# Seven block products in place of eight in both up projections, with GpSimd making the low parts of the weight blocks and their sums

## The chip, the cores and the metric

One core of one Trainium2 chip runs the whole program. The metric is the device time of one execution in microseconds: 2602.4 us before the change (median of 3 runs, 2601.3 to 2602.51).

## The reference, cut to what matters

The program computes two transformer-like blocks, one behind the other, on 1024 tokens of width 1024. The change touches the two feed-forward parts, the first of the first block and the second of the second:

```python
def _conv_ffn(h, w_up, conv_w, conv_b, w_down):      # h: 1024 x 1024, w_up: 1024 x 5632
    up = h @ w_up
    up = causal_depthwise_conv_width_3(up, conv_w) + conv_b
    val, gate = jnp.split(up, 2, axis=-1)
    return (jax.nn.silu(gate) * val) @ w_down

def conv_ffn(h, w_up, conv_w, conv_b, w_down, grid_rows):
    a, g = jnp.split(h @ w_up, 2, axis=-1)           # 2816 columns each
    a = dwconv3x3(a as 16 rows of 64 tokens, conv_w) + conv_b
    return (jax.nn.gelu(a, approximate=False) * g) @ w_down
```

## The kernel before, in words

Activations lie transposed, 128 features on the partitions and tokens along the free axis. A large product is made from bf16 parts: each fp32 matrix is split into a high part (rounded to bf16) and a low part (the rest), and `PASSES` multiplies high by high, high by low and low by high (line 189), three matmuls of 128 x 128 weights by 512 tokens for each 128 rows of the inner dimension. The moving parts of the normed input lie in `hT`.

**The up projection** (`Ffn`, line 1978) runs 22 units. Unit j makes 128 features of the first half of the columns (s = 0) and 128 of the second (s = 1), for 1024 tokens in two halves: four PSUM banks of a unit, two units in turn. A unit is 4 x 8 x 3 = 96 matmuls. Its weights (1 MB, two DMAs issued by SyncE, SP) come into one raw buffer; ScalarE (ACT) makes the high parts (L2051), VectorE (DVE) the low parts (L2084), into one of two buffers, and only then is the raw buffer loaded again. GpSimd (POOL) does nothing in it.

Behind the matmuls of a unit ACT writes the centre tap with bias out of PSUM (L2127, L2156), DVE adds the other taps one after another (`conv_causal`, L2137, four of them; `conv_grid`, L2170, eight), ACT applies Silu or Gelu (L2147, L2179), DVE multiplies (L2149, L2181), ACT writes the high part of the gated product (L2063) and DVE the low part (L2097). Each engine runs its list in order; `act_unit` and `dve_unit` (L2053, L2086) write the order out, and loops (`Fori`) run over pairs of units. PE starts the first halves of units 0 and 1 while the norm of the second token half is still being made (`pe_first_half`), and then their second halves (`pe_rest`). The norm (`Norm`, L512) scales on DVE (L693), shifts and rounds on ACT (L643), and subtracts on DVE (L705); the scaled values of the second feed-forward live in four small rotating buffers.

**The down projection** (`DownByHalves`, L1821) follows: 16 units of 22 x 3 = 66 matmuls. Unit 0's raw weights are loaded while the up projection ends (`load_first`), unit 1's and all later ones' into the region of `hT` when the up projection has read it. One raw buffer again: SP issues unit u's load when unit u-1's low part is made (L1872), ACT and DVE split it (L1893, L1899). Units 0 and 1 run their first 21 of 22 row blocks, then wait for the last unit of the up projection. `update` adds the product to the residual `xT`, which stays in place all the time.

Of the kernel before, what the change touches and what calls it, by code (L numbers as in the profile page):

```python
# [111 lines left out]
ARENA = 31488  # L112


class Kernel:


    def __init__(self, nc, ins, out, ctx):
# [393 lines left out]
class Norm:  # L512
# [85 lines left out]
    def act_square(self, act, i, a, b, t):  # L598
# [4 lines left out]
        if self.dst is None and self.split is not None and i == self.tiles:  # L603
            act.wait_ge(self.ready, self.tiles)
# [82 lines left out]
    def dve_scale(self, dve, i, n, a, b, t):  # L687
# [3 lines left out]
        if self.dst is None and t >= 4:  # L691
            dve.wait_ge(self.ready, i - 3)
# [1127 lines left out]

class DownByHalves:  # L1821
# [6 lines left out]
    def __init__(self, k, w_name, gate, second_banks=4):  # L1828
# [19 lines left out]
    def first_splits(self):  # L1848

        n = FT - 1 - self.FIRST  # L1850
        return [(self.raw_first[0], self.w_even[0]), (self.raw_first[1][:, 0:n, :], self.w_even[1][:, :, 0:n, :]),
                (self.raw_first[1][:, n:, :], self.last_row)]

    def first_hi(self, act, f):

        act.wait_ge(self.first_loaded, 32)
        act.wait_ge(f.made[0], FT // 2 + 1)
        for i, (raw, parts) in enumerate(self.first_splits()):
            if i == 1:
                act.wait_ge(f.done[0], FT // 2 + 1)  # L1860
# [1951 lines left out]
```

## Time and profile before

| what | before |
|---|---|
| median of 3 runs | 2602.4 us |
| span of the profiled execution, first to last instruction | 2597.6 us |
| what lies around the span, taken against the median | 4.8 us |
| PE busy | 2484.4 us (96%) |
| DVE, ACT, POOL busy | 1622.0, 886.6, 26.8 us |
| up projection 1, units 2 to 21 | 541 to 955.1 us |
| up projection 2, units 2 to 21 | 1928.1 to 2342.8 us |

The profile gives no time of the profiled execution but its span; the 4.8 us around it are the difference from the median. PE is TensorE's matmul queue; L200 is the matmul line of the helper `split_matmuls`, L1917 that of the down projection.

### The profile page before, as it was taken

What the parts mean: (1) busy time and instruction counts of PE and PEld (TensorE: products, weight loads), DVE (VectorE), ACT (ScalarE), POOL (GpSimd) and SP (SyncE); (2) the same over time, 40 slices, a digit from 0 to 9 for tenths busy, and PEclk for the clock granted to TensorE, in tenths of its full rate; (3) what the DMA queues carried; (4) which work ended last, traced back from release to release, by engine and by line L of the source; (5) the groups of instructions that cost most, each with busy time, mean ns of one, the idle gap of its engine ahead of it and who ended that gap; (6) DMA issues with size and microseconds to landing.
All of it is one profiled execution on the core that took longest, in us unless ns stands there. A gap on an engine that the chain in (4) does not pass through costs nothing. (4 is left out here: it accounts for less than half of the span.)

```text
span 2597.6 us, 39539 instructions
## 1 busy us (share of the span) xinstructions
PE 2484.4 (96%) x16809; PEld 1336.3 (51%) x16809; DVE 1622.0 (62%) x2112; ACT 886.6 (34%) x1061; POOL 26.8 (1%) x60
## 2 busy tenths in 40 slices
PE   7999889999999999999999999979989999999997
PEld 4457664444444444444767776764434444444443
DVE  6688747544444443645477878786766777774243
ACT  5118316332233232323354544452332222222121
POOL 0010000010000000000000000000000000000000
PEclk9999999999999999999999999999999999999999
DMA  9127563111111124343210000021101211113442
GB/s 328 31 73 235 192 212 131 33 49 49 48 48 48 48 77 111 106 120 130 56 31 18 25 26 25 18 97 50 33 17 52 61 49 48 48 55 106 112 112 87
DMA packets 302918, 207.37 MB, mean 80 GB/s; under 512 B 11296, under 2 KB 298174, under 8 KB 302143
## 3 DMA queue, kind: packets, MB, share of 16 engines
q1 hardware_dynamic: 301910, 205.08, 26.3%
q8 instruction: 105, 1.72, 0.3%
q10 hardware_dynamic: 873, 0.32, 0.1%
q14 instruction: 30, 0.25, 0.0%
HBM read 191.22 MB, written 13.64 MB: 79 GB/s over the span
## 5 line engine op out<-in xcount | busy, mean ns | idle before, releaser
L200 PE MATMUL ps<-hT,arena 128*128 128x512 bf16 (+1 forms) x6240 | 1337.3, 376 | 13.3 <-DVE hT L705 4.9
L200 PEld LDWEIGHTS ps<-hT,arena 128*128 128x128 bf16 x6240 | 609.1, 98 | 739.0 <-issue 17.1
L1917 PE MATMUL ps<-arena 128*128 128x512 bf16 x2112 | 458.7, 379 | 3.0 <-DVE arena L1899 3.0
L1917 PEld LDWEIGHTS ps<-arena 128*128 128x128 bf16 x2112 | 206.3, 98 | 252.2 <-DVE arena L1899 5.3
L2170 DVE SCALAR_TENSOR_TENSOR arena<-ps,vec,arena 128x945 f32<-128x945 f32 (+2 forms) x176 | 215.1, 1222 | 70.1 <-ACT arena L2156 50.7
L2137 DVE SCALAR_TENSOR_TENSOR arena<-ps,vec,arena 128x1023 f32<-128x1023 f32 (+1 forms) x88 | 106.8, 1276 | 177.8 <-ACT arena L2127 177.8
L1899 DVE TENSOR_TENSOR arena<-hT,arena 128x2816 bf16<-128x2816 f32 (+2 forms) x44 | 93.7, 2157 | 164.8 <-ACT arena L1893 164.6
L1893 ACT ACTIVATE arena<-hT 128x2816 bf16<-128x2816 f32 (+2 forms) x44 | 77.8, 1798 | 240.1 <-DMA hT<-w_down_dram 112.6
L2988 PE MATMUL ps<-arena 128*128 128x128 f32 (+1 forms) x896 | 103.2, 272 | 21.6 <-DVE arena L3309 21.6
L2084 DVE TENSOR_TENSOR arena<-hT,arena 128x2048 bf16<-128x2048 f32 x44 | 100.9, 2292 | 28.1 <-ACT arena L2051 27.8
L2988 PEld LDWEIGHTS ps<-arena 128*128 128x128 f32 (+1 forms) x896 | 98.5, 187 | 25.6 <-DVE arena L3309 24.0
L2127 ACT ACTIVATE arena<-ps,vec 128x1024 f32<-128x1024 f32 x44 | 50.6, 1200 | 173.5 <-PE ps L200 173.5
L2179 ACT ACTIVATE arena<-arena 128x1024 f32<-128x1024 f32 x22 | 23.2, 1056 | 227.5 <-DVEq L2174 227.5
L2097 DVE TENSOR_TENSOR arena<-arena 128x1024 f32 (+1 forms) x44 | 53.9, 1225 | 59.9 <-ACT arena L2063 59.9
L2051 ACT ACTIVATE arena<-hT 128x2048 bf16<-128x2048 f32 x44 | 83.3, 1894 | 8.1 <-DMA hT<-w_up_dram 8.1
L3326 DVE COPY_PREDICATED arena<-masks,ps 128x512 f32<-128x512 uint32 x56 | 49.9, 890 | 56.1 <-PE ps L2988 55.4
L3128 ACT ACTIVATE arena<-arena 128x1024 f32<-128x1024 f32 x56 | 58.4, 1053 | 73.7 <-DVE arena L3300 53.0
L3073 ACT ACTIVATE arena<-ps 128x1024 f32<-128x1024 f32 (+1 forms) x48 | 36.2, 755 | 123.9 <-PE ps L200 112.2
L605 ACT ACTIVATE arena<-xT 128x512 f32<-128x512 f32 x64 | 39.8, 630 | 110.9 <-DVE xT L568 54.0
L200 PE MATMUL ps<-arena,hT 128*128 128x128 bf16 (+1 forms) x1152 | 76.0, 228 | 0.9 <-PEq L160 0.9
L200 PEld LDWEIGHTS ps<-arena,hT 128*128 128x128 bf16 x1152 | 72.9, 98 | 3.7 <-issue 1.2
L1068 PE MATMUL ps<-arena 128*128 128x512 f32 x160 | 71.6, 599 | 1.7 <-ACT arena L645 1.1
(421 smaller groups left out, 2468.9 us busy)
## 6 DMA issues: line engine op xcount, KB each, us to landing
xT<-ada_w_dram SPq DMA_DIRECT2D x24, 1024.0 KB, 5.9
hT<-w_up_dram SPq DMA_DIRECT2D x44, 512.0 KB, 5.0
hT<-ffn_up_dram SPq DMA_DIRECT2D x44, 512.0 KB, 5.0
hT<-w_down_dram SPq DMA_DIRECT2D x30, 704.0 KB, 7.1
hT<-ffn_down_dram SPq DMA_DIRECT2D x30, 704.0 KB, 6.9
arena<-w_in_dram SPq DMA_DIRECT2D x33, 512.0 KB, 3.9
xT<-w_mod_dram SPq DMA_DIRECT2D x16, 1024.0 KB, 6.1
arena<-w_mod_dram SPq DMA_DIRECT2D x8, 1024.0 KB, 19.2
```

The source lines that it names most:

```text
L200: last = pe.matmul(out, lhs(a, kt), rhs(b, kt, i), start=start and kt == 0 and (a, b) == (0, 0), stop=stop and kt == n_k - 1 and (a, b) == ...
L1068: last = pe.matmul(k.ps[:, 2 * p + half, :], exact[n][:, kt, :], h[:, kt, half * HALF:(half + 1) * HALF], start=kt == 0, stop=kt == KD - 1)
L1893: last = act.activation(parts[0], raw, ACT.Copy)
L1899: last = dve.tensor_tensor(parts[1], raw, parts[0], ALU.subtract)
L1917: last = pe.matmul(self.bank(u), self.part(u, a, kt), self.g[:, b, kt, cols], start=kt == 0 and (a, b) == (0, 0), stop=kt == FT - 1 and (a ...
L2051: act.activation(self.w[:, b, :, 0], self.raw, ACT.Copy).then_inc(self.hi[b], 1)
L2084: dve.tensor_tensor(self.w[:, b, :, 1], self.raw, self.w[:, b, :, 0], ALU.subtract).then_inc(self.lo[b], 1)
L2097: dve.tensor_tensor(self.g[:, 1, 2 * i + b, :], c[0], self.g[:, 0, 2 * i + b, :], ALU.subtract).then_inc(self.done[b], 1)
L2137: last = eng.scalar_tensor_tensor(c[s][:, lag:T], p[s][:, 0:T - lag], w[:, tap, s, bass.ds(j, 1)], c[s][:, lag:T], ALU.mult, ALU.add)
L2170: eng.scalar_tensor_tensor(to, src[:, r0 + di:r1 + di, c0 + dj:c1 + dj], w[:, 3 * (di + 1) + dj + 1, bass.ds(j, 1)], to, ALU.mult, ALU.add ...
L2988: return pe.matmul(out[rows, columns], chunk[:, rows], chunk[:, columns], start=True, stop=True)
L3128: act.activation(v, v, ACT.Exp).then_inc(exp_done, 1)
```

## The change

Both up projections become classes of their own, `CausalFfn` and `GridFfn`, on a common `Ffn`, with every loop written out. Units 0, 1 and 2 stay plain (96 matmuls). From unit 3 on (`PLAIN = 3`, 19 units) the 256 x 1024 weights and the 1024 x 1024 input are taken as 2 x 2 blocks, and the four output banks are made by seven block products of 4 x 3 matmuls each, 84 in all, by Winograd's form: three sums of weight blocks (S1, S2, S4), one difference in place of a block (S3), and four combinations of input blocks (T1 to T4), made once. Partial results are passed on inside PSUM: ACT copies the bank of product 1 over the next bank (`seed_12`), copies that one on after product 6 (`seed_21`), keeps product 5 in SBUF, and DVE adds it twice (`finish_22`, `finish_12`). TensorE makes product 4 of unit u behind product 1 of unit u+1. GpSimd makes T1 to T4 of both norms from the normed values, which now stay whole in SBUF (`place`), and for each of the 19 units the four sums of weight blocks and both low parts. `xT` is stored to HBM before the up projection, its place holds the convolution's buffers and T1 and T2, and it is loaded back when the up projection ends.

```diff
+    def load(self, sp, u):                     # one raw buffer
+        if u >= 1:
+            sp.wait_ge(self.a_lo, u)
+        for s in range(2):
+            sp.dma_start(self.raw[...], self.src[u, s]).then_inc(self.loaded, 16)
+    def sync(self, sp, down):
+        for u in range(2, FT):
+            self.load(sp, u)
+        sp.wait_ge(self.a_lo, FT)
+        sp.wait_ge(self.s_lo, FT - self.PLAIN)
+        down.load_first(sp)
+        sp.wait_ge(self.made, FT)
+        down.load(sp, 1)
+        sp.dma_start(self.k.xT[:, 0:4, :], self.x_mid[:, 0:4, :]).then_inc(down.x_home, 16)
+        sp.wait_ge(self.done, FT)
+        sp.dma_start(self.k.xT[:, 4:KD, :], self.x_mid[:, 4:KD, :]).then_inc(down.x_home, 16)
...
+        for u in range(self.PLAIN, FT):        # PE; product: 12 matmuls
+            pe.wait_ge(self.a_lo, u + 1)
+            pe.wait_ge(self.free0, u - 1)
+            self.product(pe, c11, u, self.A11, ...).then_inc(self.multiplied_out, 1)
+            if u > self.PLAIN:
+                fourth_product(u - 1)          # waits for added (22) of u-1
+            pe.wait_ge(self.s_lo, n)
+            pe.wait_ge(self.free1, u - 1)
+            self.product(pe, c22, u, self.S1, ..., True, range(0, 2))
+            pe.wait_ge(self.copied, self.copy_count(u, "1 to 12"))
+            self.product(pe, c12, u, self.S2, ...).then_inc(self.multiplied_out, 1)
+            self.product(pe, c11, u, self.A12, ..., False)
+            self.product(pe, c22, u, self.S1, ..., False, range(2, 4)).then_inc(self.multiplied_out, 1)
+            pe.wait_ge(self.copied, self.copy_count(u, "12 to 21"))
+            self.product(pe, c21, u, self.S3, ..., False).then_inc(self.multiplied_out, 1)
+            self.product(pe, c12, u, self.S4, ..., False).then_inc(self.multiplied_out, 1)
...
+    def pool(self, pool, norm):
+        pool.wait_ge(norm.normed, 2 * KD)
+        pool.tensor_tensor(self.t1, v12, v11, ALU.subtract).then_inc(self.combined, 1)
+        pool.tensor_tensor(self.t2, v22, self.t1, ALU.subtract).then_inc(self.combined, 1)
+        pool.tensor_tensor(v11, self.t2, v11, ALU.subtract).then_inc(self.combined, 1)
+        pool.tensor_tensor(v21, v21, self.t2, ALU.subtract).then_inc(self.combined, 1)
+        for u in range(self.PLAIN, FT):
+            pool.wait_ge(self.loaded, 32 * (u + 1))
+            pool.tensor_tensor(sums[:, 0], raw[:, self.A21], raw[:, self.A22], ALU.add).then_inc(self.summed, 1)
+            pool.tensor_tensor(raw[:, self.S3], raw[:, self.A11], raw[:, self.A21], ALU.subtract).then_inc(self.summed, 1)
+            pool.tensor_tensor(sums[:, 1], sums[:, 0], raw[:, self.A11], ALU.subtract).then_inc(self.summed, 1)
+            pool.tensor_tensor(sums[:, 2], raw[:, self.A12], sums[:, 1], ALU.subtract).then_inc(self.summed, 1)
+            self.lo_a(pool, u)                 # 128x2048, behind ACT's hi_a
+            self.lo_s(pool, u)                 # 128x1536, behind ACT's hi_s
...
+    def act(self, act, down):
+        self.hi_t(act, 1)                      # T1's high part; waits for both spills
+        self.hi_t(act, 2)
+        for u in range(FT):
+            if self.strassen(u):
+                act.wait_ge(self.added, self.added_count(u, 12))
+            else:
+                act.wait_ge(self.made, u + 1)
+            self.first_centre(act, u)
+            if self.strassen(u + 1):
+                self.seed_12(act, u + 1)
+            act.wait_ge(self.made, u + 1)
+            self.second_centre(act, u)
+            if u + 2 < FT:
+                self.hi_a(act, u + 2)          # waits for made(u) and for the sum S3 of u+2
+            if self.strassen(u + 2):
+                self.hi_s(act, u + 2)
...
+            if self.strassen(u + 1):
+                self.seed_21(act, u + 1)
+            self.activate(act, u)
+            if self.strassen(u + 1):
+                self.keep_p5(act, u + 1)
+            act.wait_ge(self.multiplied, u + 1)
+            act.activation(self.g[:, 0, u, :], self.conv_of(u, 0), ACT.Copy).then_inc(self.g_hi, 1)
+    def dve(self, dve, down):
+        self.lo_t(dve, 1)
+        for u in range(FT):
+            if self.strassen(u):
+                self.finish_12(dve, u)
+            self.taps(dve, u)
+            if 2 <= u + 2 < self.PLAIN:
+                self.lo_a(dve, u + 2)
+            if u == FT - 2:
+                down.first_lo(dve)
+            if u == FT - 1:
+                down.split_lo(dve, 1)
+            dve.wait_ge(self.acted, u + 1)
+            self.multiply(dve, u)
+            if u == 0:
+                self.lo_t(dve, 2)
+            if self.strassen(u + 1):
+                self.finish_22(dve, u + 1)
+            dve.wait_ge(self.g_hi, u + 1)
+            dve.tensor_tensor(self.g[:, 1, u, :], ...).then_inc(self.done, 1)
+            if u == 0:
+                self.lo_t(dve, 3)
+            if u == self.PLAIN - 1:
+                self.lo_t(dve, 4)
```

In the stages, `f.load` and `f.spill` (2 MB of `xT` to `x_mid` for each token half) stand in SP's list behind the mixer's weights, and `down.update` waits for `x_home`. GpSimd's building of the masks of a later stage moves behind the first down unit.

## Rows read from the trace of the kernel before

**Rows 1.** The page: busy time of each engine, share of the span, instructions.

```profile
PE 2484.4 (96%) x16809; PEld 1336.3 (51%) x16809; DVE 1622.0 (62%) x2112; ACT 886.6 (34%) x1061; POOL 26.8 (1%) x60
```

**Rows 2.** The page: the chain that ended last, shares of the span by line.

```profile
PE ps L200 19%; PE ps L1917 7%; DVE arena L2170 1%; DMA hT<-ffn_down_dram 1%; PE ps L589 1%; PE ps L3530 1%; DVE arena L1899 0%; ACT arena L1893 0%; PE ps L3572 0%; DVE arena L693 0%; DVE hT L3702 0%; DVE arena L2084 0%; DVE hT L705 0%; ACT
```

**Rows 3.** The chain of waits in order of time: start us, us, what.

```profile
1949.10 393.87 PE ps L200 x1824
```

**Rows 4.** Two stretches: length, busy us (times) by engine, granted clock, DMA share, GB/s.

```profile
541.00:955.11 414.11, 414.11 (x1920) 187.72 (x1919) 194.41 (x144) 126.03 (x103) 0.00 (x0) 1.00 0.19 52
...
1900.00:1907.00 7.00, 6.12 (x16) 1.45 (x17) 7.00 (x12) 3.96 (x6) 0.00 (x0) 0.59 0.01 2
```

**Rows 5.** GpSimd's groups by shape: busy us, mean ns of one, idle before.

```profile
L2617 POOL TENSOR_SCALAR_AFFINE_SELECT masks<-masks 128x64 f32<-128x64 f32 x28 | 9.9, 352 | 1.9
...
L1056 POOL MEMSET arena<- 128x7168 f32 x1 | 6.1, 6076 | 89.3 <-PE ps L1083 89.3
...
L1040 POOL MEMSET arena<- 64x1 f32 x1 | 0.1, 92 | 0.1
```

**Rows 6.** VectorE's groups by shape.

```profile
L2170 DVE SCALAR_TENSOR_TENSOR arena<-ps,vec,arena 128x945 f32<-128x945 f32 x88 | 105.7, 1202 | 59.0 <-ACT arena L2156 50.7 <-DVE arena L2170 1.4
...
L2084 DVE TENSOR_TENSOR arena<-hT,arena 128x2048 bf16<-128x2048 f32 x44 | 100.9, 2292 | 28.1 <-ACT arena L2051 27.8
...
L2097 DVE TENSOR_TENSOR arena<-arena 128x1024 f32 x36 | 44.1, 1225 | 50.9 <-ACT arena L2063 50.9
...
L705 DVE SCALAR_TENSOR_TENSOR hT<-arena,mod,hT 128x512 bf16<-128x512 f32 x48 | 34.7, 747 | 0.0
...
L1717 DVE TENSOR_TENSOR arena<-ps,arena 128x512 f32<-128x512 f32 x4 | 2.8, 688 | 4.5 <-PE ps L1572 4.5
```

**Rows 7.** ScalarE's groups by shape.

```profile
L2051 ACT ACTIVATE arena<-hT 128x2048 bf16<-128x2048 f32 x44 | 83.3, 1894 | 8.1 <-DMA hT<-w_up_dram 8.1
...
L2156 ACT ACTIVATE arena<-ps,vec 128x1024 f32<-128x1024 f32 x22 | 26.5, 1204 | 70.4 <-PE ps L200 70.4
...
L2179 ACT ACTIVATE arena<-arena 128x1024 f32<-128x1024 f32 x22 | 23.2, 1056 | 227.5 <-DVEq L2174 227.5
...
L643 ACT ACTIVATE hT<-arena,mod 128x512 bf16<-128x512 f32 x64 | 45.2, 719 | 36.5 <-DVE arena L693 36.5
...
L1379 ACT ACTIVATE arena<-ps 128x512 f32<-128x512 f32 x28 | 15.2, 594 | 10.4 <-PE ps L1329 10.4
```

**Rows 8.** The page: DMA issues, times, KB each, median us from issue to landing.

```profile
hT<-ffn_up_dram SPq DMA_DIRECT2D x44, 512.0 KB, 5.0
...
hT<-w_down_dram SPq DMA_DIRECT2D x30, 704.0 KB, 7.1
...
xT<-x_kept SPq DMA_DIRECT2D x2, 4096.0 KB, 13.0
```

**Rows 9.** Timeline, start of up projection 2: start us, us, engine, line [idle before].

```profile
1906.13 2.07 DVE L705 SCALAR_TENSOR_TENSOR hT<-arena,mod,hT 128x512 bf16<-128x512 f32 x3
...
1914.30 1.21 ACT L2156 ACTIVATE arena<-ps,vec 128x1024 f32<-128x1024 f32 x1 [7.33 <-PE ps L200]
...
1915.54 10.03 DVE L2170 SCALAR_TENSOR_TENSOR arena<-ps,vec,arena 128x945 f32<-128x945 f32 x8 [7.33 <-ACT arena L2156]
...
1928.06 57.25 PE L200 MATMUL ps<-hT,arena 128*128 128x512 bf16 x263 [3.44 <-DVE arena L2084]
```

**Rows 10.** Timeline, start of down projection 1.

```profile
955.11 57.14 PE L1917 MATMUL ps<-arena 128*128 128x512 bf16 x264
...
962.89 2.55 ACT L1893 ACTIVATE arena<-hT 128x2816 bf16<-128x2816 f32 x1 [5.28 <-DMA hT<-w_down_dram]
...
965.48 3.09 DVE L1899 TENSOR_TENSOR arena<-hT,arena 128x2816 bf16<-128x2816 f32 x1 [2.98 <-ACT arena L1893]
...
976.27 2.64 ACT L1893 ACTIVATE arena<-hT 128x2048 bf16<-128x2048 f32 x2 [4.18 <-DMA hT<-w_down_dram]
...
1013.01 14.42 PE L1917 MATMUL ps<-arena 128*128 128x512 bf16 x66 [0.75 <-DVE arena L1899]
```

More of the change, by code:

```diff
@@ L602, in act_square @@
             act.wait_ge(self.centred, i + 1)
[L603 removed]
+        if self.dst is None and self.place is None and self.split is not None and i == self.tiles:
             act.wait_ge(self.ready, self.tiles)
@@ L1856, in first_hi @@
         act.wait_ge(self.first_loaded, 32)
[L1857 to L1860, printed above, removed]
+        act.wait_ge(f.made, FT - 1)
+        for raw, parts in self.first_splits():
             act.activation(parts[:, 0], raw, ACT.Copy).then_inc(self.first_hi_done, 1)
@@ new lines, in place, with bank, both, conv_of @@
+    def place(self, t, half):
+        return self.v[t // 4][half][:, t % 4, :]
+    def bank(self, u, s, half):
+        return self.k.ps[:, 4 * (u % 2) + 2 * s + half, :]
+    def both(self, u, s):
+        first = 4 * (u % 2) + 2 * s
+        return self.k.ps[:, first:first + 2, :].rearrange("p b n -> p (b n)")
+    def conv_of(self, u, s):
+        return self.conv[:, 2 * (u % 2) + s, :]
+    def p5_copy(self, u):
+        return self.conv_of(u, 1)[:, HALF:T]
+    def strassen(self, u):
+        return self.PLAIN <= u < FT
@@ new lines, in plain_part, with lhs, pe_first_half @@
+    def plain_part(self, pe, u, half, s, before=None):
+        def lhs(part, kt):
+            return self.stationary(u, 2 * s + kt // 4, part, kt % 4)
+        return split_matmuls(pe, [self.bank(u, s, half)], lhs,
+                             lambda part, kt, _: self.b_part(kt // 4, half, part, kt % 4), KD, before=before)
+    def pe_first_half(self, pe, wait_parts, after):
+        for u in range(2):
+            pe.wait_ge(self.a_lo, u + 1)
+            for s in range(2):
+                self.plain_part(pe, u, 0, s, (lambda kt: wait_parts(pe, 0, kt)) if u == s == 0 else None)
+                after(u, s)
@@ L2177, in finish_gelu, with hi_a @@
-def finish_gelu(k, engine, eng, c, p, g, sem):
-    if engine == "scalar":
-        eng.activation(c[0], c[0], ACT.Gelu).then_inc(sem, 1)
-    else:
-        eng.tensor_tensor(g, c[0], p[1], ALU.mult).then_inc(sem, 1)
+    def hi_a(self, act, u):
+        act.wait_ge(self.loaded, 32 * (u + 1))
+        if u >= 2:
+            act.wait_ge(self.made, u - 1)
+        if self.strassen(u):
+            act.wait_ge(self.summed, self.sum_count(u, "S3"))
+        act.activation(self.w[:, u % 2, 0, 0:4], self.raw, ACT.Copy).then_inc(self.a_hi, 1)
@@ L2267, in _ @@
             out.sync(sp, 2)
+            f.load(sp, 0)
+            for half in range(2):
+                sp.wait_ge(out.read, KD * (half + 1))
+                f.spill(sp, half)
+                if half == 0:
+                    f.load(sp, 1)
             f.sync(sp, down)
@@ L2603, in _ @@
         def _(pool):
-            pool.wait_ge(norm.ready, 2 * KD)
+            f.pool(pool, norm)
+            pool.wait_ge(down.first_lo_done, 3)
+            pool.wait_ge(down.made, 1)
             pool.memset(k.masks[:, :, :, :], 0.0).then_inc(masked, 1)
```

521 lines of the change are left out of this document (304 added, 217 removed).

## The prediction

> **What bounds the kernel now.** I read the page's busy times first: PE is busy 2484.4 of 2597.6 us, and POOL 26.8 [rows 1]. Then the chain of waits by line: its largest piece is L200, the split matmuls [rows 2]. In order of time one link of it is the whole of up projection 2 behind its start: 1824 matmuls in 393.87 us without another engine between them, 0.2159 us each, 20.7 us for a unit of 96 [rows 3]. The windows say the same of up projection 1: PE is busy all of 541 to 955.11, at full granted clock, while DVE has 194 and ACT 126 of 414 us [rows 4]. So both up projections are bound by the number of matmuls, and GpSimd has nothing to do in them.
>
> **Matmuls removed.** 19 units lose 12 matmuls in each projection: 456 x 0.2159 = 98.5 us. Weights, shapes and moving widths stay, so I take the same time for each. This holds only while PE never waits in a unit, which is now 84 x 0.2159 = 18.1 us long.
>
> **GpSimd's price.** No row has a two-input operation on POOL. Below: a memset, one write stream, takes 6076 ns for 7168 elements, 0.85 ns each, with about 0.1 us fixed [rows 5]. Above: the affine select takes 352 ns for 64 elements, (352 - 92) / 64 = 4.1 ns each [rows 5]. I take three streams (two read, one written) at the memset's pace, 2.5 ns, since the dense memset is nearer in shape than a strided select of 64: 1.4 us for 512 elements, 3.9 for 1536, 5.2 for 2048.
> The Trainium skill (GPSIMD Engine Reference, Performance versus the Vector engine) gives 4497 ns for a tensor_tensor of 2048 fp32, beside 2293 ns on VectorE. The trace has 2292 ns for VectorE's [rows 6]; no row shows GpSimd's. By that figure the sum below would be about 2 us lower.
>
> **A unit on GpSimd.** 4 x 1.4 + 5.2 + 3.9 = 14.7 us busy. Its chain is longer, for there is one raw buffer: low part made, load (5.0 us to landing for each half, the second issued 0.5 later, 5.5 [rows 8]), four sums 5.6, low part 5.2, handovers 0.5: 16.8 us of 18.1. ACT's high part (1.9 us [rows 7]) fits beside the last two sums, and the 3.9 us low part of the sums beside the load. It is hidden with 1.3 us to spare; the limit is (18.1 - 6.5) / 4096 = 2.8 ns an element.
>
> **A unit on DVE and ACT, grid form.** Count from the end of product 3. DVE adds bank 12 (0.7, [rows 6], L1717), ACT's centre 1.2, eight taps 10.03 [rows 9], Gelu 1.06, multiply 1.2, ACT's high part 1.06, DVE's low part 1.23, handovers 0.6: 17.1 of 18.1. The other addition of product 5 (0.7) lies beside ACT's high part; DVE gave up the 2.3 us L2084 [rows 6]. The waits put on PE: seed_12 is ready at 3.4 (product 1 ends at 2.6, copy 0.6 [rows 7]), needed at 6.5; seed_21 follows product 6 (9.1) and is done by 9.9, in the causal form behind second centre, hi_a and hi_s by 10.6, needed at 12.9; bank 22 is added at 16.4, needed at 20.7. Behind a late hi_a queue seed_21, the activation and keep_p5, and PE for them: 2.3 us cover that. The causal form has four taps and some 9 us of DVE work. So I count both projections at zero stall per unit.
>
> **Start of up projection 2.** The spills (2 MB for each half) go when the residual is final and end while the norm runs; loads of units 1 and 2 stand behind them in SP's list, with over 10 us to spare. New on the path is GpSimd's T chain: the normed values are complete at 1906.2 (beside the last L705 [rows 9]); T1 and T2 take 5.3 each, 1916.8; ACT's four pieces of T2's high part at 0.72 [rows 7] 1919.8, and only behind them stands unit 0's centre, before at 1914.30. Centre 1.2, taps 10.0, low part of unit 2's weights 2.3: PE begins unit 2 at 1933.6 in place of 1928.06 [rows 9]: +5.5. With memset's pace +0, with the select's +12. In projection 1 unit 0 ends some 10 us later against the norm, so +0.5 (0 to 2). T4's low part stands on DVE behind unit 2's gated product and ahead of product 4 of unit 3: +1.3 (0 to 3).
>
> **The hand-over to down.** Let E be the end of up; the table of before is [rows 10], with E = 955.11. Unit 1's load, high and low parts are unchanged: ready at E + 13.5. Then unit 2's load went at once and its low part was ready at 982.2, with 983.6 needed (132 matmuls): 1.4 us to spare. Now SP first waits for done(22), the last gated low part, at E + 13.5 + multiply, high, low part and handovers 3.9 = E + 17.4, then issues 2 MB of xT, and only then the load. 4 MB of xT take 13.0 us, two pieces of unit weights 7.1 [rows 8]: landed at E + 17.4 + 6.5 + 7.1 less some 1 of overlap = E + 30.0, split 5.8, ready at E + 35.8 against 28.5: +7.3 for each projection. Below, were the two transfers side by side at no cost, +2.3; above, +8.3. The first half of xT goes behind unit 1's load and is home at E + 15, needed at 28. The lost 1.4 us come up again at unit 4, where PE waited 0.75 us for a load that stood behind 1 MB of others [rows 10]: +1.3 each (0 to 1.5). The masks now built behind down's first unit are needed long after. PE's clock: behind the idle before 1900.4 the grant was 0.59 for 7 us [rows 4]; the new stalls of 7 us may bring such a stretch, +0.5 each, 0 to 3.
>
> **Sum.** -98.5 + 0.5 + 5.5 + 1.3 + 14.6 + 2.6 + 1.0 = -73.0. The span would be 2524.6; the median lies 4.8 above the span, so 2529.4, and I say 2529. Lower ends: -98.5 + 4.6 = -93.9, 2508.5. Upper ends: -98.5 + 2 + 12 + 3 + 16.6 + 3 + 6 = -55.9, 2546.5.
>
> **Rivals.**
> *GpSimd becomes the bound.* Place: the chain load, sums, low part. Above 2.8 ns an element, each further ns costs 4096 x 38 units = 156 us. At 3.3 ns the whole gain of 73 us is gone; halfway between 2.8 and the select's 4.1 the time is 2529 + 0.65 x 4.096 x 38 = 2630, at 4.1 2731. For it: only the select's row. Against: the select's shape is strided and tiny. This is the case that ends slower than before. Chance 0.11, of which 0.08 above 2607.
> *DVE and GpSimd get in each other's way.* Here GpSimd is busy 14.7 of 18.1 us beside DVE for the first time. DVE's grid cycle has 1.0 us to spare. Were its gated low part (two SBUF inputs) to wait for the end of a running 3.9 us low part on GpSimd, the cycle would be 21.0, +2.9 a unit; GpSimd waiting for DVE's two such operations of 1.23 in the causal form stretches 16.8 to 19.3, +1.2. All units: 19 x 4.1 = 78; by my table GpSimd's low part ends at about 16.4, when DVE's would begin, so half is a fair price: 2568. The splits at the start of up 2 (three L705, [rows 9]) would wait 5 us more. Chance 0.2.
> The Trainium skill (SBUF — State Buffer, SBUF: two separate sides) has this as a rule: an operation of VectorE with two SBUF inputs and one of GpSimd that reads SBUF hold the shared port pair in turn, each for the whole instruction. No row shows the two at work together. By it the time would be this rival's, 2568, and without it the forecast's.
> *The reload is hidden.* If neither the 2 MB nor SP's wait delays unit 2 of down, 14.6 + 2.6 + 1.0 fall away: 2511. For it: DMA is little used there. Against: SP's order. Chance 0.12.
> *My forecast*: 0.54, own range 2508 to 2547. Others 0.03.
>
> **Numbers.** The runs of before spread 1.2 us; 0.2% is 5.2 us, about what a measurement tells from no change. Faster 0.88, same 0.02, slower 0.10. 8 in 10: from 2506 (reload hidden) to 2580 (half of the contention and some).
>
> **What would show it.** PE without gaps from unit 3 on, in groups of 84 x 0.216; POOL tensor_tensor of 2048 at 4 to 6 us; GpSimd idle between the low part of the sums and the landing of the load; PE idle some 7 us ahead of down unit 2 with xT's load before it in the DMA list. Wrong if POOL's mean is over 5.8 us, if DVE's low part L2097 has 3 us ahead of it, or if PE waits on seed_21.

## The result

The changed kernel takes 2530.86 us (median of 4 runs, 2528.72 to 2536.26); the kernel before took 2601.85 us beside it. The ratio is 0.9732 [0.9717, 0.9746]. Five more runs later gave 2533.47 us, ratio 0.9737 [0.9724, 0.9750]. The forecast was 2529, with 2506 to 2580 as the range. In the experiments below one run of low_on_dve, at a granted clock of 0.65 where its others have 0.98, took 3608.7 us and enters no figure. The profiled span fell from 2597.6 to 2529.2 us, by 68.4.

### The profile after

The page of the changed kernel: busy times, three of its groups on GpSimd, and the loads of down 1.

```profile
PE 2392.4 (95%) x16353; PEld 1293.0 (51%) x16353; DVE 1655.4 (65%) x2158; ACT 1018.4 (40%) x1219; POOL 566.6 (22%) x296
...
L2189 POOL TENSOR_TENSOR arena<-arena 128x2048 f32<-128x2048 f32 x2 | 12.5, 6274 | 1144.7 <-DVE arena L696 1144.7
...
L2180 POOL TENSOR_TENSOR arena<-arena 128x2048 bf16<-128x2048 f32 x38 | 155.1, 4082 | 103.9 <-ACT arena L2172 103.9
...
L2184 POOL TENSOR_TENSOR arena<-masks,arena 128x1536 bf16<-128x1536 f32 x38 | 135.8, 3574 | 0.0
...
hT<-w_down_dram SPq DMA_DIRECT2D x30, 704.0 KB, 7.7
```

PE lost 92 us of busy time against [rows 1], and POOL rose from 26.8 to 566.6. L2180 (low part of the blocks) and L2184 (low part of the sums) are new on GpSimd. The mean of 3574 ns for 1536 elements is a mix: 3.1 us undisturbed, 4.1 where VectorE worked beside it.

The chain of waits in order of time has the piece that answers to [rows 3]:

```profile
1938.49 326.53 PE ps L2109 x1512
```

That is 0.2160 us a matmul over 18 units with no other engine in it: 84 matmuls, 18.14 us a unit. Where the span fell and where it lost is read from PE's timeline, here of projection 1 and the first down units (start, length, in brackets the idle time before and what ended it):

```profile
579.67 2.76 PE L2109 MATMUL ps<-hT,arena 128*128 128x512 bf16 x12 [1.95 <-DVE hT L2241]
...
906.02 13.76 PE L1923 MATMUL ps<-arena 128*128 128x512 bf16 x63
920.32 13.77 PE L1923 MATMUL ps<-arena 128*128 128x512 bf16 x63 [0.54 <-DVE arena L1907]
...
942.79 30.90 PE L1923 MATMUL ps<-arena 128*128 128x512 bf16 x132 [7.40 <-DVE arena L1907]
974.01 14.42 PE L1923 MATMUL ps<-arena 128*128 128x512 bf16 x66 [0.32 <-DVE arena L1907]
```

The wait of 1.95 us is for T4's low part (L2241). Down unit 2 waits 7.40 us, where [rows 10] have no wait before unit 4; unit 4 starts 67.99 us after the first down matmul (974.01 - 906.02), before 57.90. What ended these waits is a conversion on VectorE, and that one waited for a load. So look at the loads, on SyncE's queue and ScalarE:

```profile
923.78 0.34 SPq L2089 DMA_DIRECT2D xT<-x_mid_w_up  x1
924.16 19.73 SPq L1881 DMA_DIRECT2D hT<-w_down_dram  x4
...
936.99 2.55 ACT L1902 ACTIVATE arena<-hT 128x2816 bf16<-128x2816 f32 x1 [13.19 <-DMA hT<-w_down_dram]
```

SP issues the x_mid reload (2 MB, the second half of the residual `xT`) at 923.78, when the last gated low part is made (done(22)), and unit 2's load right behind it. The load's second half lands 12.3 us after its issue (12.6 in down 2), against a median of 7.7; the reload ahead of it lands after 7.2. Start of up projection 2, engine by engine:

```profile
1867.33 6.28 POOL L2189 TENSOR_TENSOR arena<-arena 128x2048 f32<-128x2048 f32 x1 [910.17 <-DVE arena L696]
1873.68 4.53 POOL L2191 TENSOR_TENSOR arena<-arena 128x2048 f32<-128x2048 f32 x1
1878.29 6.47 POOL L2194 TENSOR_TENSOR arena<-arena 128x2048 f32<-128x2048 f32 x1
...
1867.16 2.07 DVE L708 SCALAR_TENSOR_TENSOR hT<-arena,mod,hT 128x512 bf16<-128x512 f32 x3
1869.15 4.48 DVE L2308 TENSOR_TENSOR masks<-mod 128x4 f32<-128x4 f32 x1
1875.65 4.71 DVE L2238 TENSOR_TENSOR xT<-arena,xT 128x2048 bf16<-128x2048 f32 x1 [2.02 <-ACT xT L2217]
...
1881.93 10.03 DVE L2396 SCALAR_TENSOR_TENSOR xT<-ps,vec,xT 128x945 f32<-128x945 f32 x8 [1.57 <-ACT xT L2379]
1892.10 2.29 DVE L2180 TENSOR_TENSOR arena<-arena 128x2048 bf16<-128x2048 f32 x1
...
1878.24 2.56 ACT L2226 ACTIVATE xT<-arena,mod 128x512 bf16<-128x512 f32 x4 [2.69 <-POOL arena L2191]
1880.71 1.19 ACT L2379 ACTIVATE xT<-ps,vec 128x1024 f32<-128x1024 f32 x1
...
1894.45 23.46 PE L200 MATMUL ps<-hT,arena 128*128 128x512 bf16 x96 [8.80 <-DVE arena L2180]
```

T1 takes 6.28 us and T2 4.53. Then follow T2's high part, behind it unit 0's centre (1880.71), ten microseconds of taps and unit 2's low part. PE waits 8.80 us, before 3.44 [rows 9].

The two engines hold each other. VectorE's L2308 has four elements a partition and takes 4.48 us: it ends at 1873.63, with GpSimd's T1 at 1873.61. T1 itself, of the same shape as T2, took 1.75 us more: VectorE's three L708 ran beside its start, until 1869.2. The next pair does the same: L2238 (2.29 us alone) ends 2.15 us behind T2, and L2194, issued at 1878.29, takes 6.47; in t_chain_later below, where no L2238 runs beside it, it takes 4.56.

The windows behind the two kinds of wait (length, then busy time of PE, PEld, DVE, ACT, POOL, granted clock, DMA share, GB/s):

```profile
942.79:946.00 3.21, 3.21 (x8) 1.19 (x9) 2.05 (x3) 0.00 (x0) 2.62 (x10) 0.50 0.55 120
946.00:950.00 4.00, 4.00 (x16) 1.62 (x15) 0.00 (x0) 0.00 (x0) 3.23 (x12) 0.83 0.93 260
...
1894.45:1900.00 5.55, 5.55 (x14) 2.04 (x15) 5.40 (x7) 4.44 (x6) 0.00 (x0) 0.53 0.67 189
```

After 7.40 and 8.80 us of idle PE, the granted clock is 0.50 and 0.53, near the level of 1.2 GHz, where steady units have 1.00, that of 2.4 GHz. Down 2 repeats down 1 (waits 7.56 and 0.42, unit 4 at +68.12 in place of +59.2).

### The profile page after: what moved, and what is told of

It reads as the page before. It is cut to its first block and busy times, and to the rows that moved or that the text cites. A ratio compares the mean times of both kernels' runs of the same rounds, so it can differ in the third digit from the quotient of the medians.

```text
span 2529.2 us, 38163 instructions
## 1 busy us (share of the span) xinstructions
PE 2392.4 (95%) x16353; PEld 1293.0 (51%) x16353; DVE 1655.4 (65%) x2158; ACT 1018.4 (40%) x1219; POOL 566.6 (22%) x296
## 5 line engine op out<-in xcount | busy, mean ns | idle before, releaser
L200 PE MATMUL ps<-hT,arena 128*128 128x512 bf16 (+1 forms) x2592 | 551.2, 373 | 19.4 <-DVE arena L2180 8.8
L2109 PE MATMUL ps<-hT,arena 128*128 128x512 bf16 x2280 | 505.2, 379 | 4.4 <-DVE hT L2241 4.4
L1923 PE MATMUL ps<-arena 128*128 128x512 bf16 x2106 | 462.5, 382 | 17.8 <-DVE arena L1907 17.8
L200 PEld LDWEIGHTS ps<-hT,arena 128*128 128x128 bf16 x2592 | 252.6, 98 | 315.9 <-issue 19.5
L2109 PEld LDWEIGHTS ps<-hT,arena 128*128 128x128 bf16 x2280 | 222.8, 98 | 274.0 <-DVE hT L2241 5.4
L1907 DVE TENSOR_TENSOR arena<-hT,arena 128x2816 bf16<-128x2816 f32 x30 | 92.8, 3093 | 221.3 <-ACT arena L1902 221.3
L2396 DVE SCALAR_TENSOR_TENSOR xT<-ps,vec,xT 128x945 f32<-128x945 f32 (+2 forms) x176 | 215.1, 1222 | 31.2 <-ACT xT L2379 25.7
L2109 PE MATMUL ps<-xT,arena 128*128 128x512 bf16 x912 | 209.3, 379 | 0.0
L2180 POOL TENSOR_TENSOR arena<-arena 128x2048 bf16<-128x2048 f32 x38 | 155.1, 4082 | 103.9 <-ACT arena L2172 103.9
L2360 DVE SCALAR_TENSOR_TENSOR xT<-ps,vec,xT 128x1023 f32<-128x1023 f32 x88 | 112.8, 1282 | 64.1 <-ACT xT L2345 62.0
L2109 PEld LDWEIGHTS ps<-xT,arena 128*128 128x128 bf16 x912 | 89.2, 98 | 107.6
L2184 POOL TENSOR_TENSOR arena<-masks,arena 128x1536 bf16<-128x1536 f32 x38 | 135.8, 3574 | 0.0
```

Of the source, the lines that this page charges most:

```text
L200: last = pe.matmul(out, lhs(a, kt), rhs(b, kt, i), start=start and kt == 0 and (a, b) == (0, 0), stop=stop and kt == n_k - 1 and (a, b) == ...
L1907: dve.tensor_tensor(parts[1], raw, parts[0], ALU.subtract).then_inc(self.lo, 1)
L1923: last = pe.matmul(self.bank(u), self.part(u, a, kt), self.g[:, b, kt, cols], start=kt == 0 and (a, b) == (0, 0), stop=kt == FT - 1 and (a ...
L2109: last = pe.matmul(out, self.stationary(u, block, a, kt), moving(b, kt), start=start and kt == 0 and (a, b) == (0, 0), stop=kt == 3 and (a ...
L2180: eng.tensor_tensor(self.w[:, u % 2, 1, 0:4], self.raw, self.w[:, u % 2, 0, 0:4], ALU.subtract).then_inc(self.a_lo, 1)
L2184: pool.tensor_tensor(self.w[:, u % 2, 1, 4:7], self.sums, self.w[:, u % 2, 0, 4:7], ALU.subtract).then_inc(self.s_lo, 1)
```

## The experiments

Twelve kernels ran, each timed beside the kernel before. The stretches are differences of starts on PE in the profiled run of each: up 1 and up 2 from the first unit of seven products to the first down matmul, down 1 from there to the first transposes, which stand behind its unit 4, down 2 from there to the first down matmul behind its first transposes (they stand later, in unit 8), and start 2 from the first matmuls of up 2's second halves to its unit 3.

| kernel | median us | ratio [95%] | up 1 | down 1 | start 2 | up 2 | down 2 |
|---|---|---|---|---|---|---|---|
| changed | 2530.9 | 0.9732 [0.9717, 0.9746] | 346.6 | 82.2 | 56.3 | 347.1 | 130.0 |
| changed_again | 2533.5 | 0.9737 [0.9724, 0.9750] | 346.6 | 82.1 | 56.1 | 350.1 | 131.1 |
| reload_late | 2517.0 | 0.9672 [0.9659, 0.9685] | 348.3 | 74.0 | 56.1 | 350.1 | 121.7 |
| t_chain_later | 2536.9 | 0.9753 [0.9740, 0.9766] | 348.8 | 82.6 | 51.9 | 351.6 | 131.5 |
| t4_earlier | 2527.3 | 0.9715 [0.9701, 0.9728] | 344.9 | 82.5 | 56.0 | 344.5 | 130.9 |
| all_three | 2508.3 | 0.9651 [0.9638, 0.9664] | 346.5 | 73.2 | 51.9 | 345.6 | 121.5 |
| best | 2517.8 | 0.9680 [0.9666, 0.9693] | 344.9 | 73.0 | 59.5 | 347.4 | 122.5 |
| late_in_up2 | 2510.1 | 0.9652 [0.9639, 0.9665] | 344.9 | 74.3 | 52.2 | 346.5 | 122.0 |
| idle_filled | 2536.4 | 0.9750 [0.9734, 0.9766] | 348.3 | 84.8 | 55.9 | 349.9 | 129.9 |
| low_on_dve | 2535.9 | 0.9748 [0.9729, 0.9768] | 346.1 | 82.6 | 56.0 | 350.4 | 130.8 |
| sums_beside_load | 2563.3 | 0.9859 [0.9842, 0.9875] | 371.0 | 82.5 | 56.0 | 352.6 | 130.9 |
| sums_in_chain | 2624.5 | 1.0088 [1.0071, 1.0104] | 391.0 | 82.3 | 55.9 | 391.9 | 130.4 |
| eighth_repeated | 2623.9 | 1.0093 [1.0077, 1.0108] | 393.7 | 81.7 | 55.1 | 393.7 | 128.5 |

Stretches that no edit touches wander: the mixing stage starts at 383.1 to 389.6 us, and the stages between down 1 and up 2 take 871 to 875. Up 1 and up 2 wander too: reload_late and idle_filled change nothing in them and have 348.3 and about 350 where the first profile has 346.6 and 347.1 (changed_again, below, shows why). A single span therefore tells no difference under some 5 us; a stretch tells more, but not 1.7 us in up 1 or 3 us in up 2.

**reload_late.**

```diff
     def sync(self, sp, ahead_of=None):         # of the down projection
-        for u in range(2, 2 * KD):
+        for u in range(3, 2 * KD):
...
         sp.dma_start(self.k.xT[:, 0:4, :], self.x_mid[:, 0:4, :]).then_inc(down.x_home, 16)
+        sp.wait_ge(down.lo, 1)
+        down.load(sp, 2)
         sp.wait_ge(self.done, FT)
         sp.dma_start(self.k.xT[:, 4:KD, :], self.x_mid[:, 4:KD, :])
```

> One edit on the changed kernel: SyncE issues unit 2's down load as soon as unit 1's low part has freed its buffer, ahead of the reload of x_mid's second half and of the wait for the gated rows that stood before it. Theory (the in-order queue holds the load, and the idle time of TensorE costs clock on top): the waits of 7.40 and 7.56 us before down unit 2 fall to under 1 us, since the load could start at 920.3 in place of 924.2 and alone takes 7.7 in place of 12.6 us; the slow clock after them (about 2.4 us each) goes too; unit 4 gets back a wait of some 1.3 us each. Sum: 17 us off the span, 2529.2 to about 2512, median about 2514, ratio to before 0.966. Rival 1 (the wait is the load's own length plus both conversions, the order doesn't matter): no change, 0.973. Rival 2 (the idle time goes, the slow clock stays since it comes from elsewhere): 12 us off, 0.968. Rival 3 (the wait moves on to unit 3 or 4): under 6 us off.

Measured 16.5 us off the two down stretches, 13.9 off the median. SP's queue and what PE waits for now:

```profile
923.48 1.10 SPq L1881 DMA_DIRECT2D hT<-w_down_dram  x2
926.96 1.23 SPq L2091 DMA_DIRECT2D xT<-x_mid_w_up  x1
...
937.76 29.30 PE L1923 MATMUL ps<-arena 128*128 128x512 bf16 x132
968.81 14.42 PE L1923 MATMUL ps<-arena 128*128 128x512 bf16 x65 [1.75 <-DVE arena L1907]
```

Unit 2 starts without a wait at 937.76 and runs into unit 3. Unit 4 comes 59.74 us after the first down matmul, with a wait of 1.75, up from 0.32. The order on the queue made the stall. The load's landing, counted from the first down matmul, came 8.2 us sooner: 3.8 because its issue no longer waits for done(22), and 4.4 because its second half lands 7.9 us after its issue and not 12.3, with the reload behind it. No run parts the two.

**t_chain_later.** In `act` and in `dve`:

```diff
-        self.hi_t(act, 1)
-        self.hi_t(act, 2)
+        act.wait_ge(self.spilled, 32)
...
                 self.hi_s(act, u + 2)
+            if u == 0:
+                self.hi_t(act, 1)
+                self.hi_t(act, 2)
...
-        dve.wait_ge(self.apart_set, 1)
-        self.lo_t(dve, 1)
...
                 self.lo_a(dve, u + 2)
+            if u == 0:
+                self.lo_t(dve, 1)
```

> One edit on the changed kernel: the high and low parts of T1 and T2 are made behind unit 0's taps and unit 2's weight parts, not ahead of them. Theory: the 8.80 us of TensorE before unit 2 of the second up projection come from first_centre(0), which stands at 1880.7 behind the conversion of T2 that waits for GpSimd, though unit 0 was multiplied by about 1873; moved, the taps end near 1884.5 and unit 2's low part near 1887, so the wait falls to 1 to 2 us, and the slow clock of unit 2 (2.6 us) goes: 9 us off (6 to 10.5), none of it in the first up projection; median about 2522, ratio 0.9695. Rival (GpSimd, busy with its four products of 2048 elements a partition until 1889.2, holds VectorE's low part up until then, as it held the 128x4 instruction for 4.3 us): the wait stays at 4 to 6 us, 3 to 5 us off, median 2526 to 2528.

The start gained 4.4 us (PE waits 3.9 before unit 2), not 9: unit 0 is done some 2 us later than I had read, and centre, taps and low part (1.2 + 10.0 + 2.7) follow. Up 2 took 351.6 us, 4.5 more than changed and 1.5 more than changed_again (new waits of 1.6 and 1.0 in unit 3, T4's wait 4.15 with slow matmuls behind it). Up 1 took 2.2 more, of which runs without this edit show 1.7. By the median it gains nothing alone.

**t4_earlier.** In `dve`, behind the taps (and no longer behind the gated tile's low part):

```diff
+            if u == self.PLAIN - 1:
+                self.lo_t(dve, 4)
             if u == FT - 2:
...
-            if u == self.PLAIN - 1:
-                self.lo_t(dve, 4)
```

> One edit on the changed kernel: VectorE makes T4's low part right behind the taps of unit 2, not after the low part of the gated tile. Theory: the waits of 1.95 and 2.46 us before the fourth product of unit 3 go, nothing else is late: 4.4 us off, median 2526.5, ratio 0.9711. Rival (GpSimd's low parts run beside it there and stretch it to over 4 us, and the multiply and the 22 sum behind it come late in their turn): 0 to 2 us off, with a new wait of a product on the 22 sum.

4.3 us off the two up stretches, 3.6 off the median. Both waits before unit 3's fourth product are gone from PE's timeline, so the theory holds; the difference of the medians is near the least that they tell.

**all_three.** The three edits together.

> The three edits together. If each of the three takes its own wait off TensorE's path, the gains add: 17 + 9 + 4.4 = 30 us off, span about 2499, median about 2500.5, ratio to before 0.961. Rival (a wait that one edit removes hides part of another's): the sum of the single gains less over 3 us. In the trace TensorE then has no wait of over 3 us within either feed-forward block from its first up unit to down unit 4, and the clock of the start of unit 2 (down and up) stays at 1.00.

22.5 us off the median in place of 30. This is the fastest kernel of the study, ratio 0.9651. PE's wait before up unit 2 is 3.9 us, as in t_chain_later, and T4's waits are gone. What the late T chain is worth here is not shown, since no run has the other two edits without it: the start is 4.1 us shorter than in t4_earlier, while up 1 and up 2 are 1.6 and 1.1 longer.

**sums_in_chain, sums_beside_load.** The same four sums of 512 elements by unit, in two places:

```diff
+            for i in range(4):                      # sums_in_chain: ahead of the first block sum
+                pool.wait_ge(self.combined, 4 + 4 * n + i)
+                pool.tensor_tensor(sums[:, 0], raw[:, self.A21], raw[:, self.A22], ALU.add).then_inc(self.combined, 1)
+            pool.wait_ge(self.combined, 8 + 4 * n)
...
             self.lo_s(pool, u)
+            if u < FT - 1:                          # sums_beside_load
+                pool.wait_ge(self.s_lo, n + 1)
+            for i in range(4 if u < FT - 1 else 0):
+                pool.wait_ge(self.combined, 4 + 4 * n + i)
+                pool.tensor_tensor(sums[:, 0], sums[:, 1], sums[:, 2], ALU.add).then_inc(self.combined, 1)
+                if i == 3:
+                    pool.wait_ge(self.combined, 8 + 4 * n)
```

> The changed kernel with four more sums of 512 elements a partition on GpSimd in every unit of seven products, ahead of the first block sum (the first sum made four times over): +5.1 us of GpSimd's work by unit, 12.3 to 17.4 of the 18.1 us that TensorE takes. Theory (what counts is the chain around the one buffer of weights: load 6.5 us to landing, sums 5.1, low part of the blocks 4.1, and so on: 15.7 us a unit): the chain becomes 20.8 us, over 18.1, so 19 units lose 2.7 us each in either projection less some 6 us of lead: up 1 and up 2 from unit 3 on take about 392 us in place of 347, span +90 (75 to 100), ratio about 1.007. Rival (GpSimd bounds only by its busy time, 17.4 of 18.1): no change, 0.973.

> The same four more sums by unit, but behind the low part of the sums, where GpSimd waits for the next load. Theory of the chain: the load lands 6.5 us after the low part of the blocks; low part of the sums 3.1 and four sums 5.1 are 8.2 to 9.2, so the cycle is 17.4 of 18.1: no change (within 3 us of 2530.9, ratio 0.973). Rival (GpSimd's busy time bounds it, or its load on the memory port that VectorE shares): slower by 20 us or more, as much as the run with the sums in the chain.

In the chain: 391.0 and 391.9 against the 392 expected. A steady unit is 20.3 us (from 715.74 to the next one's start at 736.02), a little less than the 20.8 forecast; the first unit waits longer, 8.0 us in up 1. GpSimd still idles for the load in every unit, ACT makes the high part of the sums when GpSimd's last sum is there, copies a bank for PE behind it, and PE waits for that copy:

```profile
715.74 5.32 POOL L2204 TENSOR_TENSOR masks<-arena 128x512 f32<-128x512 f32 x4 [1.81 <-DMA arena<-w_up_dram]
...
726.24 1.48 ACT L2176 ACTIVATE arena<-masks 128x1536 bf16<-128x1536 f32 x1 [0.58 <-POOL masks L2211]
727.63 0.58 ACT L2259 ACTIVATE ps<-ps 128x512 f32<-128x512 f32 x1
...
728.26 10.53 PE L2109 MATMUL ps<-hT,arena 128*128 128x512 bf16 x47 [2.04 <-ACT ps L2259]
```

Beside the load they cost 24.4 us in up 1 and 5.5 in up 2 (2.5 against changed_again), where I had forecast no change; the rival was nearer. GpSimd's timeline in projection 1, a whole unit without a gap:

```profile
717.49 6.19 POOL L2214 TENSOR_TENSOR masks<-masks 128x512 f32<-128x512 f32 x4
723.76 1.27 POOL L2202 TENSOR_TENSOR masks<-arena 128x512 f32<-128x512 f32 x1
724.99 1.27 POOL L2203 TENSOR_TENSOR arena<-arena 128x512 f32<-128x512 f32 x1
726.22 1.27 POOL L2205 TENSOR_TENSOR masks<-masks,arena 128x512 f32<-128x512 f32 x1
727.57 1.28 POOL L2207 TENSOR_TENSOR masks<-arena,masks 128x512 f32<-128x512 f32 x1
728.79 4.08 POOL L2180 TENSOR_TENSOR arena<-arena 128x2048 bf16<-128x2048 f32 x1
732.82 4.09 POOL L2184 TENSOR_TENSOR arena<-masks,arena 128x1536 bf16<-128x1536 f32 x1
736.99 6.18 POOL L2214 TENSOR_TENSOR masks<-masks 128x512 f32<-128x512 f32 x4
```

The unit is 19.50 us (736.99 - 717.49): the four took 6.2, not 5.1, and L2184 4.1. In projection 2 L2184 takes 3.1 and the unit 18.5, still without a gap. So both limits are real: the chain through the one buffer, and GpSimd's sum of busy time, whichever is longer. Four sums more by unit cost about 60 us more inside the chain (89.2 against 29.9).

**low_on_dve.**

```diff
+        if self.strassen(u - 1):                # the load also waits for the last sum
+            sp.wait_ge(self.summed, self.sum_count(u - 1, "S4"))
...
-            self.lo_a(pool, u)
             self.lo_s(pool, u)
...
-            if 2 <= u + 2 < self.PLAIN:
+            if u + 2 < FT:
                 self.lo_a(dve, u + 2)
```

> The low part of the weight blocks (128x2048) goes back to VectorE, behind the taps; GpSimd keeps the sums and their low part. Theory (VectorE's cycle in up 2 is 13.9 us busy of 18.1, and 2.3 us more go into the 1.2 us waits that surround the multiply): no change within 3 us, GpSimd's busy time falls by 38 x 4.1 = 155 us. Rival 1 (VectorE is the bound of the second projection, with 16.2 busy and its waits of 4.4 us: 20.5): +2.3 us x 19 = +44 in up 2, nothing in up 1. Rival 2 (VectorE's low part runs beside GpSimd's low part of the sums and is held by it, 2 us more by unit): +20 to +40 in up 2.

Up 1 is 346.1 and up 2 350.4, as changed and changed_again have it. VectorE in projection 2, then in projection 1:

```profile
2119.39 2.29 DVE L2182 TENSOR_TENSOR arena<-arena 128x2048 bf16<-128x2048 f32 x1
2121.61 1.21 DVE L2408 TENSOR_TENSOR xT<-xT,ps 128x1024 f32<-128x1024 f32 x1
...
718.57 4.12 DVE L2371 TENSOR_TENSOR xT<-xT 128x1024 f32<-128x1024 f32 x1
```

In projection 2 the low part fills VectorE's gap behind the taps. In projection 1 the multiply (1.22 alone) takes 4.12 beside GpSimd, and yet PE never waits for it. The median, 2535.9, is 2.4 us above changed_again, inside the intervals. So this low part did not have to move to GpSimd for seven products to fit.

**idle_filled.** In the down projection's `unit`:

```diff
+        if u == 2:
+            for _ in range(30):
+                pe.matmul(self.k.ps[:, 7, :], self.g[:, 0, 0, 0:P], self.g[:, 0, 1, 0:HALF], start=True, stop=True,
+                          skip_group_check=True)
         pe.wait_ge(self.lo, u)
```

> The changed kernel with 30 matmuls of 512 columns (6.5 us) to a bank that nobody reads, ahead of the wait of down unit 2 in both feed-forward blocks: the wait for the weights stays, TensorE's idle time of 7.4 and 7.6 us falls to about 1. Theory (the slow clock of unit 2's start, 0.50 to 0.53 in its first 3 to 4 us, follows from the idle time): the granted clock stays at 1.00 and 2.4 us by block come back, 4.9 us off, median 2526; the same four up waits of TensorE stay. Rival (the clock falls for another reason, or gives nothing back since the wait sets the time): no change.

No gain: 2536.4. In down 1 the clock did hold at unit 2, and the time went elsewhere:

```profile
936.00:946.00 10.00, 9.01 (x42) 3.96 (x42) 3.43 (x2) 2.55 (x1) 7.20 (x16) 1.00 0.28 78
975.00:980.00 5.00, 2.29 (x6) 0.89 (x7) 4.00 (x3) 0.00 (x0) 0.00 (x0) 0.73 0.16 45
```

```profile
945.74 14.42 PE L1923 MATMUL ps<-arena 128*128 128x512 bf16 x65 [0.93 <-DVE arena L1907]
...
977.71 2.74 PE L1923 MATMUL ps<-arena 128*128 128x512 bf16 x6 [2.81 <-DVE arena L1907]
```

The grant is 1.00 across the filled stretch, unit 2 runs at full pace, and then unit 4 waits 2.81 us in place of 0.32. It starts 69.0 us after the first down matmul, before 67.99, and the slow stretch now stands there (0.73): unit 4 takes longer, and down 1 is 84.8 us. In down 2 the filling left a wait of 2.14 us and a grant of 0.72 over the 6 us around it; unit 4 starts at 68.6 against 68.1. The chain of loads and conversions sets unit 4's start, so the slow clock behind unit 2's wait costs next to nothing there (changed has waits of 0.32 and 0.42 left at unit 4).

**best.** all_three with the late T chain in projection 2 only (T_LATE), and there

```diff
         pool.wait_ge(self.combined, 2)
+        if self.T_LATE:
+            self.lo_a(pool, 2)
...
+            if u == 0 and self.T_LATE:
+                self.lo_t(dve, 1)
+            elif u == 0:
+                self.lo_a(dve, 2)
```

> The changed kernel with three edits: unit 2's down load ahead of the reload (16.5 us off in the run of it alone), T4's low part behind the taps of unit 2 (4.3 off alone), and in the second projection alone T1 and T2 converted behind unit 0's centre, with unit 2's low part on GpSimd between T2 and T3 in place of VectorE behind the taps. Theory: in the run with T1 and T2 late, the chain to unit 2 was centre, 10.0 us of taps, 2.7 us of low part, and TensorE waited 3.9 us for it; on GpSimd the low part is done some 7 us sooner, TensorE waits only for the taps (about 1 us), and unit 3's waits of 1.6 and 1.0 us go since its load starts sooner: 10 us off at the start of up 2. Sum: 30 us off 2529.2, span about 2499, median about 2500, ratio 0.961; 8 us below the run of all three. Rival (VectorE's first instructions of the stage and the conversions are held by GpSimd's extra 4.1 us, and unit 3 waits for the low part of T2 or T3): no better than all three, 2508.

The rival was right: 9.5 us worse than all_three. PE's wait before unit 2 did fall, from 3.9 to 1.3 us. VectorE and PE at the start of up 2:

```profile
1882.35 8.70 DVE L2249 SCALAR_TENSOR_TENSOR xT<-arena,mod,xT 128x512 bf16<-128x512 f32 x4
...
1893.18 9.38 DVE L2249 SCALAR_TENSOR_TENSOR hT<-arena,masks,hT 128x512 bf16<-128x512 f32 x4
...
1878.73 20.88 PE L200 MATMUL ps<-hT,arena 128*128 128x512 bf16 x96 [1.27 <-DVEq L2413]
1912.70 2.72 PE L2112 MATMUL ps<-hT,arena 128*128 128x512 bf16 x6 [13.09 <-DVEq L2413]
```

Four low parts of 512 elements take 8.70 us, and again 9.38; undisturbed they take 2.74. One by one they are 3.67, 1.76, 1.75, 1.75, then 4.55, 3.58, 0.74 and 0.74: the first six end 0.5 to 0.6 us behind an instruction of GpSimd. So unit 1's taps are late and unit 3 waits 13.09 us.

**late_in_up2, changed_again.** The first is best without the two lines above, unit 2's low part again on VectorE behind the taps; the second is the changed kernel itself.

> All three edits again, with T1 and T2 converted late in the second projection alone (in the first one they stand as in the change), and unit 2's low part on VectorE, behind the taps. Theory (in the run before it, GpSimd's low part pushed its chain 4 us later, so that VectorE's four-part low parts of T2 and T3 met GpSimd's sums and took 8.7 and 9.4 us in place of 2.7; without it they take 2.7 to 6.8, as in the run of all three): the wait of 13.1 us before unit 3 falls to about 1.6, the one before unit 2 rises from 1.3 to 3.9, up 1 keeps the 344.9 us of the run with T4 earlier. Span 2504 to 2507, median about 2507, ratio 0.964. Rival (the 13.1 us come from the order of VectorE's work, not from GpSimd's low part): 2515 to 2520 again.

> The changed kernel itself once more, on the same chip as the run above, since its own time rests on four runs: median 2528 to 2534, ratio to before 0.972 to 0.975; the waits of TensorE as before: 7.4 and 7.6 us (down unit 2), 8.8 (up unit 2), and 2 to 4 us each before T4's product, the matmuls behind it at full or at half clock. If the half clock behind the T4 wait comes and goes from run to run, it makes 3 to 4 us of difference between runs of one kernel.

The same low parts in late_in_up2:

```profile
1883.19 2.74 DVE L2247 SCALAR_TENSOR_TENSOR xT<-arena,mod,xT 128x512 bf16<-128x512 f32 x4
...
1886.98 6.78 DVE L2247 SCALAR_TENSOR_TENSOR hT<-arena,masks,hT 128x512 bf16<-128x512 f32 x4
```

The wait before unit 3 is 1.9 us, the median 2510.1, the same as all_three within their intervals. So GpSimd's low part ahead of T3 made the 13.09 us, as expected. In changed_again T4's wait in up 2:

```profile
1937.36 4.45 PE L2109 MATMUL ps<-hT,arena 128*128 128x512 bf16 x12 [3.73 <-DVE hT L2241]
```

The wait was 2.46 us in the first profile, with 2.76 for the 12 matmuls behind it. Here it is 3.73, and they take 4.45. That is the 3.0 us between 347.1 and 350.1.

**eighth_repeated.**

```diff
+            self.product(pe, c11, u, self.A11, lambda part, kt: b(0, 0, part, kt), True)
             self.product(pe, c11, u, self.A11, lambda part, kt: b(0, 0, part, kt), True).then_inc(self.multiplied_out, 1)
```

> The changed kernel with the first product (12 matmuls) of every unit of seven made twice, the second time afresh, so that TensorE has eight products' work and all else is as in the change. Theory (the gain is the 456 matmuls and the rest of the change costs what its waits say): +98.5 us, less the waits before T4's product (1.95 and 2.46), which the longer unit covers: +94, median about 2625, ratio 1.009, that is 23 us above the kernel before: the two hand-overs to the down projection (10 and 9 us) and the start of up 2 (5.4). Rival 1 (the helpers are near their limit and unseen waits cost more in the change than the sum says): under +90. Rival 2 (the hand-over is late because the last up unit is shorter by a product, and the wait of 7.4 us goes with a longer one): +80, ratio 1.004.

+93.0 us against the changed kernel (+90.4 against changed_again), and 23.6 above the kernel before. The 7.4 us wait of down unit 2 is still there, so it does not come from the shorter unit:

```profile
992.76 30.18 PE L1923 MATMUL ps<-arena 128*128 128x512 bf16 x132 [7.41 <-DVE arena L1907]
```

## Why the prediction was right

The mechanism and nearly every term held. The terms, in us:

| step | forecast | measured |
|---|---|---|
| matmuls removed | -98.5 | -98.5 (1512 in 326.53) |
| start of up 1 | +0.5 | 0 |
| start of up 2 (wait 8.80 against 3.44) | +5.5 | +5.4 |
| T4's low part (1.95 + 2.46) | +1.3 | +4.4 |
| hand-over, waits of down unit 2 (7.40 + 7.56) | +14.6 | +15.0 |
| rest of the way to unit 4 of down (10.1 + 8.9 less 15.0) | +2.6 | +4.0 |
| slow clock behind the hand-over's waits | +1.0 | in the row above |
| slow clock at unit 2 of up 2 | 0 | +2.6 |
| down behind unit 4 | 0 | +0.7 |
| all else (the first mixing stage alone begins 2.2 us sooner) | 0 | -2.0 |
| span | -73.0 | -68.4 |

- **Matmuls.** PE never waits from unit 4 on. The run eighth_repeated isolates the term: 93.0 by the medians, where 98.5 less T4's two waits of 4.4 makes 94.1.
- **GpSimd's price.** The guess of 2.5 ns an element was high: 1.27, 3.10 and 4.08 us undisturbed for 512, 1536 and 2048, against 1.4, 3.9 and 5.2. The Trainium skill's 4497 ns for 2048 fp32 (GPSIMD Engine Reference, Performance versus the Vector engine) agrees with L2191's 4.53; with a bf16 result the trace has 4.08. The +5.4 at the start of up 2 met the forecast partly by luck: T1 and T2 were priced at 10.6 together and took 10.8, namely 4.5 each and 1.75 in which VectorE held T1. The chain of load, sums and low part was the right frame, but not the only one: sums_beside_load shows the busy sum as a second limit.
- **Hand-over.** Order of issue, as forecast: reload_late took the stall away. The forecast put the issue 17.4 us behind the first down matmul and the landing at 30.0; measured are 17.8 and 31.0. Clock and unit 4 were priced as two terms; they are one, since both lie in the chain of loads.
- **T4's low part was mis-sized**: 4.4 us in the first profile and 7.4 in changed_again, over the forecast's own upper end of 3, for 1.3. GpSimd's work holds VectorE's (in up 2 L2328 takes 1.75 and L2241 3.35 us, alone 1.22 and 2.29), and the slow clock comes on top in some runs.
- **Clock.** A slow stretch came behind the long waits (7.40, 7.56, 8.80), and cost where no chain of loads covered it: 2.6 us at up unit 2, a place that the forecast did not price.
- **Rivals.** GpSimd did not bound. DVE and GpSimd do hold each other: L2308 with four elements ended with T1, as the rule of the Trainium skill (SBUF — State Buffer, SBUF: two separate sides) has it. The taps, which read PSUM and SBUF, kept their 10.03 us beside GpSimd. In the steady state VectorE's time to spare takes the holds, for PE never waits there; so the rule holds and the price that I gave for it (39 us, 2568) did not come. The most that such pairs cost in any run is the 9.5 us of best. The reload was not hidden.
- **Median.** The forecast put it 4.8 us above the span; it was 1.7. That and a span 4.6 too low nearly cancel: had only one of the two been off, the forecast would have missed by 3 to 5 us and not by 2. That much of the agreement is luck.

## What to carry over

When a helper engine gets new work around a single buffer, work out two lengths by unit, its busy sum and its chain with the load; the longer one against PE's unit decides, and where in the chain an instruction stands matters more than how much it is. Look then at what the edit makes SyncE wait for: one wait and one 2 MB transfer ahead of a load cost 16.5 us in two places here, a sixth of what the removed matmuls gave. Keep VectorE's instructions with two inputs in SBUF apart from GpSimd's, above all short ones in a row on the way to something that TensorE waits for.

## What the runs showed that I had not expected

- Four VectorE instructions of 512 elements took 8.70 and 9.38 us beside GpSimd, 2.74 without it.
- Behind a wait of 1.96 us, 12 matmuls took 4.45 us in reload_late (granted clock 0.62) and 2.76 behind 1.95 us in the changed kernel (1.00), in the same place. What decides it is open.
- A slow clock can cost next to nothing: idle_filled removed it from unit 2 of down 1, and the time came back as a wait at unit 4.
- The holding goes both ways: GpSimd's instructions of 2048 elements took 6.3 and 6.5 us beside VectorE's, 4.5 without.
